# Attention pipeline of a two-block kernel: exponentials issued ahead of the copy of the turned probabilities on ACT

## What is computed

```python
def _masked_softmax(s, mask):
    s = jnp.where(mask, s.astype(jnp.float32), -jnp.inf)
    m = jnp.max(s, axis=-1, keepdims=True)
    e = jnp.exp(s - m)
    d = jnp.sum(e, axis=-1, keepdims=True)
    return e / jnp.where(d > 0.0, d, 1.0)
...
for l in range(DEPTH_2):                    # 2 layers
    o_a = _nsa(...)        # 8 heads of 64: compressed, selected and window attention, gated and summed
    o_b = _fox(...)        # 8 heads of 64: causal attention with a forget bias
    o_m = _memory_xattn(...)                # 4 heads of 128 over 256 memory tokens
```

## Time and profile before

| what | value |
|---|---|
| median of 3 runs | 4837.57 us (4835.1 to 4839.89) |
| the profiled execution: its time | 4835.1 us |
| the profiled execution: its span | 4833.3 us |
| PE, DVE, ACT busy over the span | 75%, 35%, 22% |
| instructions | 55361 |
| NSA stages | 3296.1 to 3406.0 and 4279.0 to 4389.0 us |
| fox stages | 3448.7 to 3504.7 and 4431.7 to 4487.7 us |
| memory stages | 3521.7 to 3548.0 and 4504.7 to 4531.0 us |

### The profile page before, as it was taken

The page is one execution under the profiler, slowest core; times in us unless marked ns, Lnnn a source line. Parts: engine busy times, 40 slices in busy tenths (PEclk is TensorE's granted clock), DMA queues, the critical chain, the costliest instruction groups (busy, mean ns, idle before and its releaser), DMA issues. The chain is left out here.

```text
span 4833.3 us, 55361 instructions
## 1 busy us (share of the span) xinstructions
PE 3630.8 (75%) x20583; PEld 2354.2 (49%) x20584; DVE 1702.5 (35%) x2770; ACT 1039.7 (22%) x1828; POOL 94.6 (2%) x183
## 2 busy tenths in 40 slices
PE   4985858585842999889999916957669659576697
PEld 1554747474732333223333305855458548454486
DVE  5315464646442111011111153245543232445432
ACT  1112121212110111111111112314432222134321
POOL 0000000000000000000000010000000000000000
PEclk8997878787865999999999958977889879768898
DMA  8141000000015698999896932320022123200131
GB/s 309 61 155 35 1 1 1 1 1 1 1 65 205 232 357 333 400 399 384 313 352 254 380 123 97 102 39 1 1 71 87 56 83 102 53 1 1 61 96 53
DMA packets 237078, 636.80 MB, mean 132 GB/s; under 512 B 27124, under 2 KB 56564, under 8 KB 235860
## 3 DMA queue, kind: packets, MB, share of 16 engines
q1 hardware_dynamic: 219618, 586.83, 33.7%
q10 hardware_dynamic: 11044, 26.07, 1.5%
q0 software_dynamic: 6224, 21.24, 1.4%
HBM read 593.97 MB, written 40.11 MB: 131 GB/s over the span
## 5 line engine op out<-in xcount | busy, mean ns | idle before, releaser
L1188 PE MATMUL ps<-raw,ex_xT 128*64 128x512 f32 x3072 | 704.4, 603 | 32.9 <-DMA raw<-in_w_dram 32.8
L1188 PEld LDWEIGHTS ps<-raw,ex_xT 128*64 128x64 f32 x3072 | 206.0, 137 | 437.6 <-issue 367.0
L1279 DVE TENSOR_SCALAR ex_gl<-ps 128x256 f32<-128x256 f32 x96 | 40.8, 425 | 1039.3 <-PE ps L1188 1039.3
L1188 PE MATMUL ps<-raw,ex_aT 128*64 128x512 f32 x1536 | 353.3, 597 | 13.9 <-DMA raw<-in_w_dram 12.9
L1188 PEld LDWEIGHTS ps<-raw,ex_aT 128*64 128x64 f32 x1536 | 104.1, 136 | 217.6 <-issue 185.2
L1503 PE MATMUL ps<-zhi,hh_z 128*128 128x512 f32 (+1 forms) x448 | 170.3, 380 | 27.8 <-DVE zlo L1572 27.8
L2008 PE MATMUL ps<-uhi,u_hh 128*128 128x512 f32 x384 | 151.5, 395 | 50.0 <-DVE ulo L2054 50.0
L663 PE MATMUL ps<-unit_x,unit_m 128*128 128x128 f32 x960 | 153.4, 313 | 46.2 <-DVE unit_xt L763 31.5
L1572 DVE TENSOR_TENSOR zlo<-oT,zhi 128x1024 fp32r<-128x1024 f32 (+1 forms) x72 | 84.5, 1174 | 267.6 <-ACT zhi L1540 267.1
L672 PE MATMUL ps<-unit_xt,unit_y 128*128 128x128 f32 x960 | 176.7, 281 | 0.0
L2054 DVE TENSOR_TENSOR ulo<-oT,uhi 128x2048 fp32r<-128x2048 f32 x36 | 82.5, 2293 | 256.9 <-ACT uhi L2031 256.9
(11 more groups left out here) (566 smaller groups left out, 6448.8 us busy)
## 6 DMA issues: line engine op xcount, KB each, us to landing
raw<-in_w_dram SPq DMA_DIRECT2D x384, 1024.0 KB, 18.3
oT<-in_w_in_dram SPq DMA_DIRECT2D x72, 512.0 KB, 3.6
mT<-in_w_ada_dram SPq DMA_DIRECT2D x12, 2048.0 KB, 17.7
oT<-in_w_in_dram SPq DMA_DIRECT2D x24, 1024.0 KB, 5.2
expert_out<-none SPq DMA_DIRECT2D x4, 4096.0 KB, 28.3
expert_out<-ex_yrow ACTq DMA_DIRECT2D x98, 128.0 KB, 6.3
modb<-in_w_in_dram SPq DMA_DIRECT2D x10, 1024.0 KB, 5.2
oT<-in_w_mem_kv_dram SPq DMA_DIRECT2D x8, 1024.0 KB, 6.6
```

The source lines that it names most:

```text
L1188: mm = pe.matmul(o, x, M["raw"][:, slot, k, h * 512:(h + 1) * 512], start=(s >= 8 and kk == 0), stop=(kk == 7))
```

## The change

In each iteration ACT issues the exponentials of unit t first and the copy of the turned probabilities of unit t-2 second. In the last two iterations, which have no exponentials, the order is as before. Nothing else is changed; buffers, semaphores and the orders of PE and DVE stay.

```diff
@@ -1866,10 +1866,10 @@
                 act.activation(Z["pT"][:, i % 2, :, 0:u["n"]], ps[:, 4:6, 0:u["n"]], ACT.Copy).then_inc(pt_out, 1)
 
             for t in range(n + 2):
+                if t < n:
+                    exponentials(t)
                 if t >= 2:
                     turned_out(t - 2)
-                if t < n:
-                    exponentials(t)
```

## The result

The changed kernel takes 4884.6 us (median of 4 runs, 4881.0 to 4885.6), the kernel before 4838.7 us (4835.1 to 4841.5). The ratio is 1.0092, with a 95% interval of 1.0080 to 1.0103: slower by 45.9 us. The forecast was slower by 28.2 us, with an upper end of 4878 us, so the sign stands and the size is wrong.

A forecast was written before the change was run, and what follows sets the result against it. The prediction took the exponentials-normalisation-maximum ring on ACT and DVE to pace the steady state, with PE slack. Losses of 14.1 us a layer, 28.2 in two, moved the median from 4837.6 to about 4865.8 us; range 4850 to 4878.

The forecast's parts named there:

- The ring: Steady-state cycle: exponentials of unit t on ACT, normalisation of t and maximum of t+1 on DVE, next exponentials; 3.92 us at NSA boundary.
- (a): Exponentials no longer stand behind a copy waiting for PE: six places in both layers, 0.7 us together, taken as 0.
- The Trainium skill's rule that the forecast weighed: Find gaps of the optimised engine, start what they wait for sooner; read for the change, up to 25 us won.
- NSA falls: NSA, keys falling from 512 to 128: later copy delays PE's chain, 0.86 us at each of three boundaries, 2.6 a stage.
- the step that was priced at 0.86: NSA boundary, from first 128-wide exponentials: copy, transposes, values and 256-key score take 4.78 us against 3.92 allowed.
- Low clock at NSA falls: PE at 1.2 GHz on the path at two of three NSA boundaries: 1.4 us each, 2.8 a stage, bounds 0 and 5.0.
- Fox falls: Fox boundaries, from first 128-wide exponentials: chain of 4.88 us against 4.14 allowed, loss 0.74 at each of three, 2.2 a stage.
- Its own sign of being wrong: Forecast wrong if maxima never wait for scores at boundaries, low-clock stretches vanish or lengthen, or stages outside attention move.
- Head of NSA: NSA start: transposes(1) wait for copy(0), 1.4 us later; ring takes over some 1.0 us late, bounds 0.9 and 1.5.
- Head of memory: Memory start: no loss, since transposes(1) stand behind a score that ends after the copy.
- Tails: Stage ends: last transposes stand behind late copy, transposes and values; NSA loses 2.7 us, fox 1.6, memory 1.2.
- Sum of a layer: Losses of the NSA, fox and memory stages in one layer added: 14.1 us; two layers 28.2 us.

The follow-up runs named there:

- the filler: Changed kernel plus 12 extra identity transposes on PE ahead of the scores of each 128-key unit in fox (three in a stage): 4867.8 us, ratio 1.0056.

## Why the prediction was wrong in size

**The ring paces the stages, PE has slack:** right. Taking the maximum out of the ring gave 46 us, a part of it by the clock.

**(a), the gain is 0 to 0.7 us:** right in that no gain shows. The copy's wait outside the tails went to zero, and nothing was won by it. The Trainium skill's rule that the forecast weighed (Perfetto Trace Analysis, Optimization Strategy) asks what the gap waits for; the gap ahead of the exponentials waited for the maximum, and moving that is what won.

**NSA falls, 2.6 us:** measured 1.3, 1.1 and 0.8 us, 3.3 us a stage. The chain is the right one: in the step that was priced at 0.86 the falls cost 1.0, 1.0 and 0.8 us, and the first group loses 0.3 us more four units later.

**Low clock at NSA falls, 2.8 us:** not seen in the profiled execution, whose falls all cost near the full-clock price. In the execution with the filler in fox, two NSA falls of the first layer cost 2.2 us each with the same NSA code, about 1.1 us more than here, and in the run with the old order in the last iteration one cost 3.8 us. So this term comes and goes. That the forecast for NSA (9.1 us) lies near the measured 7.0 us owes something to luck: it held a term that did not come.

**Fox falls, 2.2 us:** this is the step that failed. "Loss 0.74 us, three boundaries" took every duration from rows at the full clock, and so put the low clock there at nothing, without a reason. The sum left out that the late copy gathers PE's idle time into one stretch of 1.8 to 2.1 us just there, where before PE had at most 1.3 us, and PE came out of it at 1.2 GHz. The falls measured 8.3 us in the first layer and 9.8 in the second, 9.1 us a stage. At the full clock, held up by the filler or kept by chance in one fall of another run, they were 1.0 us each, so 0.7 us of the error is the sum itself (the step ahead of the priced one) and 6.2 us the clock. The forecast had the clock in its NSA terms and in the tails, and not here. Its own sign of being wrong, low-clock stretches that lengthen, was seen here. The Trainium skill (TensorE: Matmul & The Clock Gate, HAM oscillation — how this bites in real kernels) describes the pattern: a wait between bursts sends the array back to its low clock, and the next burst runs cold. The page tells of longer waits than these; the trace shows the pattern at 1.79 us of wait, with 0.50 behind it.

**Head of NSA, 1.0 us:** 0.9 measured (1.3 lost, 0.4 won back within the next two units). **Head of memory, 0:** wrong, 1.0 us. The transposes of unit 1 waited 2.2 us for the copy, then they and the value matmuls (1.92 us for four, 1.03 at the full clock) ran at the low clock ahead of the next score. I had claimed that there was no such gap in memory.

**Tails:** NSA 2.8 us (forecast 2.7), memory 1.1 (1.2), fox 2.1 in the first layer and 1.3 in the second, 1.7 in the mean (1.6).

**Sum of a layer:** forecast 14.1 us; measured 20.5 with the 0.8 us between NSA and fox. Of the 6.4 us more, fox falls give 6.9, memory's head 1.0, the stretch behind NSA 0.8 and NSA's falls 0.7; NSA's clock term takes back 2.8, and the other terms differ by 0.1 us each. In the stretch between NSA and fox the granted clock was 0.61, before 0.63; why was not tried.

## What to carry to other kernels

Before moving an instruction that waits behind another, ask who waits for it. In this pipeline the step that frees a single buffer for another engine (here the copy, and the one pair of banks) had to go out as early as it could, even with ready work behind it. Issued a unit late, it could be put back in the last iteration, which saved the tail, but not at the falls, where that blocked the exponentials. When a chain gets longer, price it again with PE's idle time gathered in one place, at 1.2 GHz as well as at 2.4, and price the step ahead of the one that looks worst. And the wait to attack is the one that the pacing ring names: here the row maximum, whose move won 46 us with two lines.

## What the runs showed that I had not expected

Twelve useless transposes three times a stage made the changed kernel faster by 17 us, since PE was busy where it had stood idle for 1.8 us, and stayed at the full clock. In fox before, PE went through waits of 1.3 us at 1.00.

The length of the wait alone doesn't settle it. One fox fall kept the full clock behind a wait of 1.97 us (the run with the old order in the last iteration). In the changed kernel PE waits 1.68 us at the first NSA fall, nearly as long as in fox, and keeps the full clock:

```profile
3327.27 1.06 PE L1821 MATMUL ps<-small,nsa_p 128*128 128x128 f32 x8 [1.68 <-ACT nsa_pT L1866]
...
3326.00:3342.00 16.00, 13.13 (x110) 8.40 (x110) 9.37 (x34) 8.86 (x28) 0.00 (x0) 1.00 0.00 1
```

In the execution with the filler in fox the same NSA code has the same waits, and 0.50 behind two of them (3327.3 and 3354.6 us); its first NSA stage is 117.3 us long instead of 115.3, the whole difference at these two falls. What decides between the two clocks was not found.
